# Scoring and picking two heads inside the query product, with gathers into rows that are free by then, and one-hots shared by three engines

## The reference, cut to what matters

```python
def peer_ffn(c, w_q, keys, U, V):          # c (288, 2048), U and V (16384, 2048)
    q = (c @ w_q).reshape(T, 8, 128)
    s1 = einsum('thd,hkd->thk', q[..., :64], keys[:, 0])
    s2 = einsum('thd,hkd->thk', q[..., 64:], keys[:, 1])
    v1, i1 = top_k(s1, 16); v2, i2 = top_k(s2, 16)
    cand = (v1[..., :, None] + v2[..., None, :]).reshape(T, 8, 256)
    vs, ic = top_k(cand, 16)
    idx = take(i1, ic // 16) * 128 + take(i2, ic % 16)
    g = softmax(vs)
    act = gelu(einsum('thkd,td->thk', U[idx], c)) * g
    return einsum('thk,thkd->td', act, V[idx])

def hybrid_layer(h, ...):
    ...                                     # mixer: h = h + mix
    c = rmsnorm(h, norm_ffn)
    h = h + peer_ffn(c, peer_w_q, peer_keys, peer_u, peer_v)
    ...                                     # gated embedding, final norm
```

## Time and profile before

| | us |
|---|---|
| median of 3 runs | 2248.26 |
| lowest and highest run | 2241.01, 2251.0 |
| the profiled execution | 2246.39 |
| its span in the profile | 2244.7 |

### The profile page before, as it was taken

How to read it: one execution, slowest core, us unless ns; L and a number is a source line. 1 busy time by engine, 2 the same in 40 slices (tenths; PEclk the granted TensorE clock), 3 DMA queues, 4 the chain that set the end, 5 groups by cost and what they waited for, 6 DMA issues and landing times. The chain is left out here.

```text
span 2244.7 us, 24655 instructions
## 1 busy us (share of the span) xinstructions
PE 1560.9 (70%) x8013; PEld 1296.3 (58%) x8013; DVE 1815.8 (81%) x2803; ACT 880.2 (39%) x1508; POOL 839.8 (37%) x593
## 2 busy tenths in 40 slices
PE   8999999889997000000222222799999999999898
PEld 6777777668997000000121122678787777777798
DVE  5588883577756999998899985699999999999676
ACT  3200003223434122212877782344444444444544
POOL 0000000000002688888677775844344444444000
PEclk9999999788997555555555555999999999999899
DMA  7234342455554999999999994299999999999363
GB/s 205 89 113 149 113 149 87 127 168 167 162 143 154 404 422 418 408 422 390 394 414 391 421 421 193 83 363 374 375 374 373 362 364 362 366 370 368 99 167 119
DMA packets 238876, 619.56 MB, mean 276 GB/s; under 512 B 26388, under 2 KB 172436, under 8 KB 180628
## 3 DMA queue, kind: packets, MB, share of 16 engines
q0 software_dynamic: 56320, 369.13, 40.8%
q1 hardware_dynamic: 182484, 249.61, 33.1%
HBM read 606.56 MB, written 12.13 MB: 276 GB/s over the span
## 5 line engine op out<-in xcount | busy, mean ns | idle before, releaser
L1432 ACT CAST v_high<-ring 128x1024 fp32r<-128x1024 f32 x256 | 269.3, 1053 | 328.9 <-DMA ring<-in_peer_v 192.0
L1602 DVE TENSOR_TENSOR v_low<-ring,v_high 128x1024 fp32r<-128x1024 f32 x256 | 310.4, 1223 | 19.5 <-ACT v_high L1432 15.6
L272 PE MATMUL ps<-low,ring 128*128 128x288 f32 x1280 | 313.6, 408 | 4.4 <-DMA ring<-in_w_in 3.4
L1279 PE MATMUL ps<-v_high,act_h 128*128 128x512 f32 x896 | 293.9, 397 | 4.3 <-ACT v_high L1432 4.0
L1279 PE MATMUL ps<-v_high,act_l 128*128 128x512 f32 x896 | 292.2, 396 | 0.0
L272 PEld LDWEIGHTS ps<-low,ring 128*128 128x128 f32 x1280 | 244.3, 191 | 72.6 <-issue 5.0
L1129 POOL DMA_INDIRECT ring<-in_peer_u,work x128 | 124.9, 976 | 401.9 <-DVE work L1504 347.5
L1254 PE MATMUL ps<-work 128*128 128x128 f32 x512 | 107.9, 378 | 236.2 <-ACT work L1380 216.7
L1262 PE MATMUL ps<-ident,work 128*128 128x128 f32 x6 | 1.8, 439 | 377.6 <-DVE work L1522 377.6
L1284 PE MATMUL ps<-v_low,act_h 128*128 128x512 f32 x896 | 253.4, 399 | 2.4 <-DVE v_low L1602 2.3
L1458 DVE CUSTOM_DVE_ANT_0 ring<-ring,ps 128x2048 f32<-128x2048 f32 x100 | 227.2, 2277 | 25.7 <-DMA ring<-in_peer_u,work 25.2
(11 more groups left out here) (431 smaller groups left out, 3625.8 us busy)
## 6 DMA issues: line engine op xcount, KB each, us to landing
ring<-in_peer_v SPq DMA_DIRECT2D x128, 1024.0 KB, 7.8
ring<-in_w_in SPq DMA_DIRECT2D x20, 2048.0 KB, 8.0
ring<-in_w_out SPq DMA_DIRECT2D x16, 1024.0 KB, 5.7
ring<-in_w_ple_gate SPq DMA_DIRECT2D x16, 1024.0 KB, 5.7
out<-work SPq DMA_DIRECT2D x37, 256.0 KB, 3.0
work<-in_state_mlstm_C SPq DMA_DIRECT2D x32, 256.0 KB, 4.9
ring<-in_peer_w_q SPq DMA_DIRECT2D x8, 1024.0 KB, 5.4
ring<-in_w_glu SPq DMA_DIRECT2D x4, 1024.0 KB, 5.1
```

Of the source, the lines that this page charges most:

```text
L272: m = pe.matmul(ps[2 * s + c][:, 0:T], ring[:, s, k * WB + c * P:k * WB + (c + 1) * P], rhs[:, k, :], start=(k == 0), stop=(k == kt - 1))
L1279: pe.matmul(ps[4 * i + 2 * hf + c], a, vh[:, hf, 512 * c:512 * c + 512], start=first and a is a_h, stop=False)
L1432: o.do(act.copy(vh[:, hf, :], vn[b % 3][:, 1024 * hf:1024 * hf + 1024]), sem("vh_done"))
L1602: o.do(v.tensor_tensor(vl[b % 3][:, hf, :], vn[b % 3][:, 1024 * hf:1024 * hf + 1024], vh[:, hf, :].bitcast(F32), ALU.subtract), sem("vl_do ...
```

## The change

It does the following.

- The key load moves on SP's queue from behind the query tiles to ahead of them. PE turns the keys after query tile 0, ACT copies them after the high parts of tile 1.
- The norm's root is made after the low and high parts of tile 1 instead of ahead of them.
- After half of tile 2, PE makes the scores of the first two heads of block 0 into banks 0 and 1. After tile 2 it turns the tokens of block 0 into banks 0 to 3. The first pick runs on DVE from there, with a step of the query product (a low part or a `copy_q`) at every third call of `beside`; then three more steps, three dot products with four steps behind each, and the rest of the product.
- Ten row buffers instead of eight, in an order written out (`turns`). Buffers 0, 1 and 2 are free at once (2 is the later place of the second block's tokens and is used once), 3 and 4 when the low parts of query tiles 6 and 7 are done, 5 and 6 after the whole product, 7 to 9 from gather 25 on. Buffer 1 leaves at gather 64.
- The other scores go two heads, then four at a time, through banks 4 to 7. The second pick begins with one dot product.
- peer_v's first three loads wait for the last reads of buffers 3, 4 and 6 (gathers 249, 250 and 252; before, 248, 249 and 251).
- For groups 32 to 63, POOL makes one `ohA` instead of two; ACT makes the third in three steps spread over three groups (distance, hat, times the gate), with a settle for each group.

```diff
-        rows = [ring[:, s // 2, ...] for s in range(4)] + [low[:, KD * T + D:KD * T + 2 * D]]
-        NR_EARLY = len(rows)
+        rows = [low[:, KD * T + D:KD * T + 2 * D], wk(O_OH, 1, D)[:, 0, :], ctok[1]]
+        rows += [ring[:, s // 2, 2048 * (s % 2):2048 * (s % 2) + 2048] for s in range(4)]
         rows += [wk(18000 + D * i, 1, D)[:, 0, :] for i in (1, 2, 3)]
+        FEW, MORE = 25, 64
+        turns = [0, 1, 2, 3, 4, 5, 6]
+        while len(turns) < FEW:
+            turns += [0, 1, 3, 4, 5, 6]
+        turns += [7, 8, 9]
+        while len(turns) < MORE:
+            turns += [0, 1, 3, 4, 5, 6, 7, 8, 9]
+        while len(turns) < 2 * P:
+            turns += [0, 3, 4, 5, 6, 7, 8, 9]
...
             def gather(n):
                 pool.wait_ge(sem("idx_ready"), n // 32 + 1)
-                if n >= NR:
-                    wait_row_read(pool, n - NR)
-                elif n == NR_EARLY:
+                if held[n] is not None:
+                    wait_row_read(pool, held[n])
+                elif turns[n] in (3, 4):
+                    pool.wait_ge(sem("low_done"), 4 * (TRIPLE["wq"][0] + 4 + turns[n]))
+                elif turns[n] in (5, 6):
+                    pool.wait_ge(sem("q_used"), 4 * sum(TRIPLE["wq"]))
+                elif turns[n] >= 7:
                     pool.wait_ge(sem("c_done"), 12)
...
             for g in range(32, 64):
-                onehots(g, (2, 3))
+                onehots(g, (3,))
...
+        def pe_query(pe):
+            for c in range(TRIPLE["wq"][1]):
+                for q in range(4):
+                    pe_quarter(pe, "wq", 0, c, c % 2, q, 9, ffn_h, ffn_l)
+                    if (c, q) == (2, 1):
+                        pe.wait_ge(sem("key_copied"), 2)
+                        pe.wait_ge(sem("tile_freed"), TRIPLE["wq"][0] + 2)
+                        pe_scores(pe, 0, 0, 2, 0)
+                if c == 0:
+                    pe.wait_ge(sem("key_in"), 16)
...
+                if c == 2:
+                    pe.wait_ge(sem("ffn_copied"), 1)
+                    pe.wait_ge(sem("scr_copied"), 2)
+                    pe_tokens(pe, 0, lambda k: (ffn_h[:, k, 0:P], ffn_l[:, k, 0:P]))
...
+            def third_onehot(g):
+                if g < 64:
+                    o.do(act.activation(far2[:, g % 4, :], iota[:], ACT.Abs, bias=nkeyA[:, 4 * g + 2:4 * g + 3]))
+                if 33 <= g < 65:
+                    o.do(act.activation(far2[:, (g - 1) % 4, :], far2[:, (g - 1) % 4, :], ACT.Relu, scale=-1.0, bias=1.0))
+                if 34 <= g < 66:
+                    if g >= 4:
+                        act.wait_ge(sem("g_done"), g - 3)
+                    o.do(act.activation(ohA[g % 2][:, 2, :], far2[:, (g - 2) % 4, :], ACT.Copy,
+                                        scale=ex3[:, 2, 4 * (g - 2) + 2:4 * (g - 2) + 3]), sem("oh_act"))
+            o.settle()
+            for g in range(32, 35):
+                third_onehot(g)
+                o.settle()
             for g in range(32, 64):
+                third_onehot(g + 3)
                 copy_gates(g)
+                o.settle()
...
-            low_parts(v, o, "wq", None, copy_q, {"tile_freed": 2}, ahead=True)
+            def query_steps():
+                for c in range(1, TRIPLE["wq"][1]):
+                    for q in range(4):
+                        ...                               # low part of quarter q of tile c
+                        yield
+                    copy_q(0, c - 1, (c - 1) % 2)
+                    yield
+                copy_q(0, TRIPLE["wq"][1] - 1, 1)
+                yield
...
+            step(4)
+            dve_root(v, o, 1)
+            step(6 + 2)
+            v.wait_ge(sem("scr_copied"), 2)
+            def beside_first():
+                if next(count) % 3 == 2:
+                    step(1)
+            pick(scr[0][:, 0:4, :], 0, beside_first)
+            step(3)
+            for n in range(3):
+                dots(n + 1)
+                step(4)
+            step(99)
             v.wait_ge(sem("cols_done"), 4)
...
-            for q in range(9):
+            for q in range(1, 9):
+                if q == 1:
+                    dots(made[0] + 1)
...
             other_tiles(sp, "out", w_out)
+            sp.dma_start(keyn, ...).then_inc(sem("key_in"), 16)
             tile_pair(sp, "wq", w_q, 0)
...
-            dve_root(v, o, 1)
             dve_peer(v, o)
```

More of the change, by code:

```diff
@@ L1192, in pool_peer, with pe_scores @@
                             sample_rows(base + j)
-        def pe_peer(pe):
[L1195 to L1202, removed]
+        def pe_scores(pe, i, h0, n, bank):
+            for j in range(n):
+                for c in range(2):
+                    at = slice(64 * c, 64 * c + 64)
+                    lhs = qpT[at, h0 + j, i * P:(i + 1) * P] if i < 2 else flat(qS[at, h0 + j])
+                    m = pe.matmul(ps[bank + c][:, j * P:(j + 1) * P], lhs, keyT[64 * c:64 * c + 64, h0 + j, :],
+                                  start=True, stop=True)
+                    if j == n - 1:
+                        m.then_inc(sem("scr_done"), 1)
@@ L1207, in pe_peer @@
             m.then_inc(sem("cols_done"), 1)
[L1209 to L1230, removed]
-                    pe.matmul(out, c_h, identr, start=True, stop=False)
-                    m = pe.matmul(out, c_l, identr, start=False, stop=True)
-                    if k % 4 == 3:
-                        m.then_inc(sem("c_done"), 1)
-            pe.wait_ge(sem("ffn_copied"), 1)
@@ L1308, in act_peer, with scores_out @@
         def act_peer(act, o):
-            high_parts(act, o, "wq", None, {}, ahead=True)
-            o.do(act.copy(identr, ident[:]), sem("ffn_copied"))
+            def scores_out(i, h0, n, bank):
+                for c in range(2):
+                    done[0] += 1
+                    act.wait_ge(sem("scr_done"), done[0])
+                    if i < 2:
+                        dst = scr[i].rearrange("p (h c) k -> p h c k", c=2)[:, h0:h0 + n, c, :]
+                        o.do(act.copy(dst, ps[bank + c][:, 0:n * PK].rearrange("p (h k) -> p h k", k=PK)), sem("scr_copied"))
+                        continue
+                    for r in range(2):
+                        q = h0 // 2 + r
+                        dst = scr[2][TS * q:TS * (q + 1)].rearrange("p (h c) k -> p h c k", c=2)[:, :, c, :]
+                        o.do(act.copy(dst, ps[bank + c][TS * q:TS * (q + 1), 256 * r:256 * r + 256]
+                                      .rearrange("p (h k) -> p h k", k=PK)), sem("scr_copied"))
@@ L1542, in dve_peer @@
                 src = scr[2] if q == 8 else scr[q // 4][:, 4 * (q % 4):4 * (q % 4) + 4, :]
-                pick(src, 2 * TK * q, every(2) if q == 1 else every(1) if q else lambda: None)
+                pick(src, 2 * TK * q, every(2) if q == 1 else every(1))
             dots(NG - 16)
```

146 lines of the change are left out of this document (95 added, 51 removed).

## The result

| | before | after |
|---|---|---|
| median of 4 runs, us | 2248.8 | 2222.82 |
| lowest and highest | 2241.01, 2251.0 | 2221.4, 2227.25 |
| the profiled execution | 2246.39 | 2223.42 |
| its span | 2244.7 | 2221.7 |

The ratio is 0.9893, with a 95% interval from 0.9869 to 0.9916: faster by 1.1%. The forecast was 2226 us with a range of 2213 to 2239. The total came out 3 us under the forecast; its terms are off by 2 to 4 us each and cancel out in part, and the interesting part is there.

What follows compares the result with a forecast made beforehand. The gather transfers were taken as the bound, with DVE 6% behind. Gathers 14, V prefetch 2 and one-hots 6 us off 2246.4 gave 2224.4, against the median 2226.3; it said 2226 us, range 2213 to 2239.

Steps and rivals of the forecast that it cites:

- the walk through the product: Query product: first gather at 672 us, dot products at 678, 683, 690, last query copy 698.5, second pick about 702.5.
- The dip: Gathers 9 to 25: DMA share dips between 740 and 760 us, one or two gaps, 4 to 8 us together.
- the signs that I had named against myself: Last query copy after 708 us, DMA share well under 0.95 in the 60 us behind it, ACT period over 1.74 us.
- Rivals 1 and 2: Product stretched to 708 us or more: 2235 us, chance 0.17; one-hots gain nothing, 5 us lost: 2237 us, chance 0.10.
- rival 4: Six-row ring: gathers wait for ACT's sums at products 11, 15, 19, 23; 2262 us at 9 us each, chance 0.05.
- Rival 3: The whole lead arrives: 21 + 3 + 8 = 32 us gained, 2216 us, chance 0.13.
- the ring: Until gather 25 only six row buffers (0, 1, 3, 4, 5, 6) take turns for the gathered rows.
- The gathers: Gather stage: 21 us of transfer lead less gaps of 4 to 8 us; 14 us gained, bounds 5 and 21.
- the transfers set the pace and the lead is kept: From the third pick on, DVE needs 2.3 us per gather, less than a transfer's 2.49, so no lead is lost.
- peer_v: 5.0 us for 2: End of the gathers: one V tile of 2.49 us stops competing with the last gathers; 2 us gained, bounds 0 and 5.
- The one-hots: Groups 32 to 63: ACT's period of 1.55 us replaces POOL's 1.74; 6 us gained, bounds -8 and 10.
- The root: Query tile 1: root after its parts removes 2.3 us of PE idling and about 1.7 us at half clock.

Runs made afterwards that it cites:

- e6: Changed kernel with row buffers 7 to 9 in use from gather 19 instead of 25 and buffer 1 given up at 40 instead of 64: 2216.17 us.
- e8: Changed kernel with ACT's exponent later, row buffers 7 to 9 from gather 19, and peer_v's first loads behind the last gathered row: 2206.33 us.
- e2: Changed kernel with the one-hot part undone: 2229.29 us, ratio 0.991 to the kernel before.
- e1: Kernel before with the one-hot part of the change alone: 2239.09 us, ratio 0.994.
- e7: Changed kernel with peer_v's first three loads held until the last gathered row has been read: 2218.77 us, ratio 0.986 to the kernel before.
- e9: Changed kernel with the norm's root ahead of query tile 1's parts again: 2223.09 us, ratio 0.9899 to the kernel before.
- e4: Changed kernel with the first three dot products moved behind the query product, gathers still early: 2226.52 us, ratio 0.9891 to the kernel before.
- e3: Changed kernel with the first gather and first three dot products held until the query product is done: 2231.37 us, ratio 0.9913 to the kernel before.

## Why the prediction was right, and where it was not

**What was right.** The bound (the transfers of the gathers), the three places where time could be gained, and the walk through the product, which is 0 to 2 us off in each of its eight events. The dip came near where it was forecast (730 to 760 us for 740 to 760) and cost 5.6 us by e6 (4 to 8 forecast). ACT became the bound of the one-hots, below POOL's old 1.74 us. That the total is 3 us off is in part luck: peer_v and the one-hots gave 6.7 us more than forecast, the gathers and the rest 5.7 us less.

**The signs and the rivals.** One of the signs that I had named against myself came up in part, through the dip: a DMA share well under 0.95 in the first 60 us behind the last `copy_q`. It is 0.91.

```profile
697.00:757.00 60.00, 20.87 (x164) 19.80 (x164) 57.93 (x108) 22.02 (x33) 34.45 (x25) 0.59 0.91 348
```

Rivals 1 and 2 fell with the last `copy_q` at 696.8 us, not 708, and the period at 1.47 us, not 1.9. Of rival 4 the place is right and the rest is not: from 715 to 765 us POOL's gathers wait 3.9 us for ACT's sums, as it says, but 11.2 us for DVE's dot products, and the gaps cost 5.6 us in all, where it needed 8.3 at each of four products. Rival 3, the whole lead, was stopped by two things, the ring and the exponent; e8, without them, has it.

**The gathers: 11.6 us for 14.** The step that failed is "the transfers set the pace and the lead is kept" from the third pick on. At gather 24 the lead was 14.8 us, inside the 13 to 17 of the walk; 4.4 us were lost at the exponent. I had counted the rates of DVE and of the transfers, and left out ACT's queue: it holds sums that free POOL's row buffers behind an exponent that waits for DVE. That order was harmless as long as picks and transfers moved together. The change moved the transfers by 15 us and the fourth pick by 9, and the rows of before (8.03 us of waiting that end 0.1 us after the product that the next sum needs) would have told it. The number itself says less than the mechanism: from gather 80 to 255 all ten kernels gain on this one execution of before, from 0.5 us (after) to 4.4 (e2), e1 with 3.3 among them. Why is open. In one stretch, 900 to 1100 us, the transfers of after ran at 402 GB/s and those of e2 at 409, at shares of 0.99 and 1.00.

**The lead's origin** was right in size and loose in reason. I started from the lead of the transfers (21 us) and took off gaps of 4 to 8. By the sum that stays at 715.5 us, the start of DVE's second pick decides: 5.6 us sooner than before and 9.1 us of dot products done make 14.7, and 14.8 was measured. The walk has that sum too, 3.8 + 9.1 = 13, and then adds the 6.5 us that DVE had waited for rows, which did not arrive.

**peer_v: 5.0 us for 2.** The mechanism was right, the term was mis-sized. I let one tile of 2.49 us leave the contest. But the start moved from 6.2 us ahead of the last issue to 0.6 us behind it, and two tiles went, 2.09 MB and 5.0 us; e7 finds another 1.9 us in the rest. The upper bound that I gave was 5.

**The one-hots: 9.7 us for 6.** Again mis-sized, in both terms. From the sixth of ACT's copies to the last, 26 groups, before takes 45.2 us and after 38.1: 7.1 us where 5 were forecast. The period is 1.477 us; my terms for it add up to 1.59, not to the 1.55 that I wrote, and the scaled copy follows Relu after 0.20 us, not 0.30. The other 2.6 us (1.8 less 0.3 to 1 forecast) lie in the first six groups, where PE's clock differs. It was granted at 0.50 up to 1396 us before, 12 us behind the first of these matmuls. In after the chain of waits has one piece of three groups at the lower level, and the clock is up by 1375 us (0.91 in 1373 to 1375 us, 1.00 behind it), 6 us behind the first:

```profile
1367.44 5.85 PE ps L1290 x24
```

I had left the lower level in place for six groups. The earlier rise goes with the shorter idle times between PE's groups, and e1, which changes nothing else, has the same 57.0 us; but in e2, with the one-hots of before, the clock rose within the first 4 us, fell and rose again (0.63, 0.80 and 0.78 in three stretches of 4 us from 1362 us on), so the reason is argued, not shown.

**The root: about 1.3 us for 4.0** (2.3 + 1.7; the key transposes, 1.1 us against it, stay where they are in e9). e9 puts the root back and DVE's later work moves by that much. I priced the root and the transposes one by one, but the transposes fill half of the root's gap, and behind the 1.15 us that are left the clock did not fall, so the 1.7 us did not arise.

**The rest: -3.3 us for 0.** It is no effect of the change that I can show: the same code takes 801.5 to 814.9 us over the eleven profiled executions.

**The issues beside DVE's subtractions.** One issue of after, at 671.85 us, falls beside three subtractions of DVE (1.89 us from 671.47 on) and takes 1.32 us; the next, with none beside it, 0.94. In e4 the first two issues fall beside such subtractions and take 1.32 and 1.31 us; in e3 the first has none beside it and takes 1.13. So 0.2 to 0.4 us go with the subtractions. The row for the first dot product says that the gather had landed 5.9 us after its issue, as before (5.8). The Trainium skill, page SBUF — State Buffer, section "Who interferes with whom", says that a DVE operation with two inputs in SBUF contends with GpSimd's reads, and that `tensor_tensor`, which these subtractions are, was not seen to stall a DMA. The trace agrees: the issue is a little longer and the landing no later.

## What to carry to other kernels

When a change moves one stream ahead of another, go through every in-order queue for an instruction that waits for the stream that was not moved, and look at what is queued behind it and who waits for that. A long wait in the trace of before that holds nobody only because two ends fall together is the next bound. Early data is worth only what the engine that consumes it can do with it in that time, so move its work as well as the transfer; and where a lead is lost, look for the stretches in which the busy resource runs dry, since each has a cause that can be undone by itself.

## What was not expected of the hardware

- Three gathers of 1 MiB delayed a weight tile of 1 MiB on another queue: in e4 it was issued 2.3 us behind the first of them and landed after 13.3 us, where the tile ahead of it took 5.5. In after, issued 9 us behind the first of them, it took 6.6.
- A single one-hot of POOL per group (128 x 128) takes 1.38 us in after, where with two per group each takes 0.91. ACT's row has no idle time in that stretch and PE's groups wait for ACT's scaled copy (0.32 us each), so POOL did not set the period; but at 1.477 us from start to start it has only 0.09 us to spare.
- The 800 us behind the first `v_high`, the same work in all kernels, took from 801.5 to 814.9 us. A change of half a per cent can't be read from one execution's span.
